# Output projections as split one-pass products, and stick-breaking sums in the scores' bank

## The reference, cut to what matters

```python
# block one, two layers
h = h + 0.5 * g1 * swiglu(mod(norm(h)), ffn1_w_in, ffn1_w_out)
z = mod(norm(h)) @ w_in
mixed = concat([o_a, o_b, o_c, o_d])     # differential attention, convolution, gMLP, forgetting attention
h = h + g2 * (mixed @ w_out)             # phase "o"
h = h + 0.5 * g3 * swiglu(mod(norm(h)), ffn2_w_in, ffn2_w_out)
# block two, two layers
proj = norm(x) @ w_in                    # q, k, v of 24 heads and three gates
y_a, y_b, y_c = o_a @ w_out_a, o_b @ w_out_b, o_c @ w_out_c      # phase "y"
merged = gates[0] * y_a + gates[1] * y_b + gates[2] * y_c
x = x + merged @ w_o                     # phase "wo"
x = x + square(relu(norm(x) @ w_up)) @ w_down
# heads c0 to c5 of block two: stick-breaking, over the keys before each query
z = q @ k.T * scale
a = exp(log_sigmoid(z) + suffix_sum(log_sigmoid(-z)))
```

## Time and profile before

| what | value |
|---|---|
| median of the runs | 2153.49 us (2151.41 to 2154.36) |
| the profiled execution's own time | 2152.88 us |
| its span | 2151.1 us |
| TensorE busy | 2051.2 us, 95% |
| mean granted TensorE clock | 0.974 of 2.4 GHz |
| GpSimd busy | 1332.5 us, 62% |

### The profile page before, as it was taken

One profiled execution on the slowest core, in us unless ns is written; L12 is line 12 of the kernel. 1 busy time (PEld: TensorE's weight loads), 2 busy tenths in 40 slices (PEclk: granted clock), 3 DMA queues, 4 the chain that ended last, 5 costly groups with the idle time before them and its releaser, 6 DMA issues.

```text
span 2151.1 us, 36602 instructions
## 1 busy us (share of the span) xinstructions
PE 2051.2 (95%) x15510; PEld 1966.5 (91%) x15510; DVE 930.2 (43%) x1761; ACT 917.4 (43%) x1393; POOL 1332.5 (62%) x612
## 2 busy tenths in 40 slices
PE   7999997999989999889999999999999999999998
PEld 4999996899989998769998999989999999988998
DVE  4554776561455477754124422144233432134223
ACT  2443454334444335434444354514544345514543
POOL 1778660477967786217887765505896765405885
PEclk8999998999989999999999999999999999999999
DMA  9997550785689775227555543335554543335552
GB/s 326 357 332 253 186 161 20 254 289 176 195 275 349 244 245 167 79 84 250 177 162 170 170 146 116 103 126 166 186 194 134 192 143 113 118 118 168 185 196 79
DMA packets 356787, 398.18 MB, mean 185 GB/s; under 512 B 8984, under 2 KB 318992, under 8 KB 356624
## 3 DMA queue, kind: packets, MB, share of 16 engines
q1 hardware_dynamic: 356464, 395.65, 55.5%
q10 hardware_dynamic: 160, 0.20, 0.0%
HBM read 394.77 MB, written 1.05 MB: 184 GB/s over the span
## 4 chain that ended last, share of the span: by engine, by line
PE 90%; DVE 5%; ACT 3%; SPq 1%; issue 1%; DMA 1%; DVEq 0%; ACTq 0%
PE bank L706 73%; PE bank L783 5%; PE bank L1108 3%; PE bank L938 1%; PE bank L805 1%; PE bank L900 1%; PE bank L1072 1%; SPq L534 1%; DVE arena L1641 1%; ACT arena L1270 1%; PE bank L697 1%; PE bank L999 1%; DVE arena L1685 1%; DMA arena<-in_ada_w 1%; PE bank L939 1%
## 5 line engine op out<-in xcount | busy, mean ns | idle before, releaser
L672 POOL TENSOR_TENSOR w_lo<-ring,w_hi 128x1024 fp32r<-128x1024 f32 (+2 forms) x608 | 1332.3, 2217 | 798.7 <-ACT w_hi L1169 798.1
L706 PE MATMUL bank<-hn,w_hi 128*128 128x256 f32 x2912 | 848.4, 291 | 26.4 <-DVE hn_lo L1578 15.8
L706 PE MATMUL bank<-hn_lo,w_hi 128*128 128x256 f32 x2912 | 832.4, 286 | 0.0
L706 PE MATMUL bank<-hn,w_lo 128*128 128x256 f32 x2912 | 832.1, 286 | 0.0
L1169 ACT ACTIVATE w_hi<-ring 128x1024 fp32r<-128x1024 f32 (+2 forms) x608 | 576.4, 975 | 485.6 <-PE bank L706 356.8
L706 PEld LDWEIGHTS bank<-hn,w_hi 128*128 128x128 f32 x2912 | 567.6, 195 | 36.7 <-issue 34.6
L706 PEld LDWEIGHTS bank<-hn_lo,w_hi 128*128 128x128 f32 x2912 | 567.8, 195 | 4.5 <-issue 3.8
L706 PEld LDWEIGHTS bank<-hn,w_lo 128*128 128x128 f32 x2912 | 567.3, 195 | 0.0
L706 PE MATMUL bank<-gated,w_hi 128*128 128x256 f32 x1408 | 249.7, 280 | 0.0
L706 PEld LDWEIGHTS bank<-gated,w_hi 128*128 128x128 f32 x1408 | 215.0, 187 | 0.0
L706 PE MATMUL bank<-gated,w_lo 128*128 128x256 f32 x704 | 196.4, 279 | 0.0
(11 more groups left out here) (188 smaller groups left out, 2130.1 us busy)
## 6 DMA issues: line engine op xcount, KB each, us to landing
ring<-in_ffn_w_in SPq DMA_DIRECT2D x88, 1024.0 KB, 6.1
ring<-in_w_in SPq DMA_DIRECT2D x72, 1024.0 KB, 5.1
arena<-in_ada_w SPq DMA_DIRECT2D x35, 2048.0 KB, 10.3
ring<-in_w_up SPq DMA_DIRECT2D x32, 1024.0 KB, 5.4
ring<-in_w_down SPq DMA_DIRECT2D x32, 1024.0 KB, 5.0
ring<-in_ffn_w_out SPq DMA_DIRECT2D x32, 768.0 KB, 4.4
ring<-in_ffn_w_out SPq DMA_DIRECT2D x32, 640.0 KB, 4.0
ring<-in_w_in SPq DMA_DIRECT2D x16, 512.0 KB, 3.6
```

The costliest lines, as they stand in the source:

```text
L672: pool.tensor_tensor(w_lo[:, q, ks], ring[:, r, k0:k0 + n], w_hi[:, q, ks], ALU.subtract) \
L706: last = mm(out, a, b, start=start and i == 0, stop=stop and i == 2)
```

## The change

- The phases o, y and wo become split products. Their chunks join the sequence of split chunks: ScalarE rounds them (8 half chunks more a phase) and GpSimd subtracts; `plain_product` goes, and `output` and `y_product` come.
- Their activations get high and low parts. In block one `mix` tiles 0 to 5 are split in pairs (`mix_high` on ScalarE, `mix_low` on VectorE) into `hn`, `hn_lo`; the outputs of fox heads and of all block two heads go from their bank to the high part by ScalarE (`pair_high`) and the low part by VectorE (in place of the copy). `merged` stays in the first branch's bank; ScalarE writes its high part (`merged_high`), VectorE its low part.
- In o and wo the first chunk goes k-tile by k-tile, and waits for each k-tile's parts. Chunks o 0 and o 1 are rounded at steps 2 and 3 of block one's heads. Wo uses banks 6, 7 and 0, 1.
- The gates are opened in two groups between the roundings of y.
- A stick head's suffix sums are added to its first scores, in banks 2 to 5 in turn; the second issue of the scores goes.

```diff
-for _part, _phases in (("one", ("f1in", "f1out", "z", "f2in", "f2out")), ("two", ("z2", "up", "dn"))):
+for _part, _phases in (("one", ("f1in", "f1out", "z", "o", "f2in", "f2out")),
+                       ("two", ("z2", "y", "wo", "up", "dn"))):
...
-            h.sb = [take("two banks", 2, f"sp {h.name}")]
+            h.sb = [take("stick banks", 4, f"copied {h.name} 0")]
             h.tp = [take("tp", SLOTS, f"sp {h.name}"), take("tp", SLOTS, f"arg {h.name}")]
-            h.pb = [take("pb", 2, f"copied {h.name} 0")]
...
+            def output(phase, i, outs, done, free=(), ready=None):
+                q = split_slot(phase, i)
+                for half, (k0, n) in enumerate(halves(phase, i)):
+                    half_ready(phase, i, half)
+                    steps = [(c, k) for k in range(n) for c in range(2)] if ready \
+                        else [(c, k) for c in range(2) for k in range(n)]
+                    for c, k in steps:
...
+                        if ready and c == 0:
+                            ready(kx)
+                        last = terms(outs[c], w_hi[:, q, half * 4 + k, ws], w_lo[:, q, half * 4 + k, ws], hn[:, kx],
+                                     hn_lo[:, kx], False, kx == 0, kx == KT - 1)
...
             def turned(hd, q, k, tile):
                 if hd.kind == "stick":
-                    (qi, ki, _, _), (pb, free) = hd.maps[0], hd.pb[0]
-                    if free:
-                        pe.wait_ge(done_by(free), eng.at(free))
-                    b, sp_ = bank[:, pb], tile[:, hd.tp[1][0], :]
-                    stick_scores(b, q, k, qi, ki, False)
+                    b, sp_ = bank[:, hd.sb[0][0]], tile[:, hd.tp[1][0], :]
                     pe.wait_ge(vector_done, eng.at(f"sp {hd.name}"))
...
+                def mix_ready(k):
+                    mark = {0: "mix parts 0", 2: "mix parts 1", 4: "mix parts 2", 6: "heads d0 2", 7: "heads d0 3"}.get(k)
...
+                def y_product(i):
+                    q = split_slot("y", i)
+                    if i == 0:
+                        pe.wait_ge(scalar_done, eng.at("z2 out 29"))
+                    if i >= 2:
+                        pe.wait_ge(vector_done, eng.at(f"merged parts {i - 2}"))
...
+                def merged_ready(k):
+                    if k % 2 == 0:
+                        pe.wait_ge(vector_done, eng.at(f"merged parts {k // 2}"))
...
+            def pair_high(heads, i, dst):
+                hd = heads[i]
+                if hd.half == 0 or hd.kind == "diff":
+                    return
+                act.wait_ge(tensor_done, eng.at(f"out {hd.name}"))
+                b = bank[:, 6 + hd.pair % 2].rearrange("p (a s) -> p a s", a=2)
+                for a in range(2):
+                    f(dst(hd)[64 * a:64 * a + 64], b[64 * a:64 * a + 64, a], ACT.Copy) \
+                        .then_inc(scalar_done, eng.step(f"high {heads[0].name} {hd.pair}" if a else None))
...
                 def between(i):
+                    if i == 0:
+                        mix_high(2, "mixed out")
+                    if i in (2, 3):
+                        round_chunk("o", i - 2)
+                    if i == 9:
+                        mix_high(0, "od normed")
...
+                        mix_high(1, "conv done")
...
+                    if i + 1 == len(Z2_BETWEEN) - 1:
+                        round_chunk("y", 0)
...
+                round_chunk("y", 1)
+                act.wait_ge(scalar_done, eng.at("z2 out 29"))
+                open_gates(0)
+                open_gates(1)
+                round_chunk("y", 2)
+                open_gates(2)
+                open_gates(3)
+                round_chunk("y", 3)
+                merged_high(0)
+                round_chunk("wo", 0)
+                merged_high(1)
+                round_chunk("wo", 1)
+                merged_high(2)
+                merged_high(3)
+                round_chunk("wo", 2)
+                round_chunk("wo", 3)
...
+                def mix_low(t):
+                    dve.wait_ge(scalar_done, eng.at(f"mix high {t}"))
+                    two = slice(2 * t, 2 * t + 2)
+                    tt(hn_lo[:, two], mix[:, two], hn[:, two], ALU.subtract).then_inc(vector_done, eng.step(f"mix parts {t}"))
+
                 def between(i):
+                    if i == 1:
+                        mix_low(2)
...
+                        mix_low(1)
+                        mix_low(0)
...
                     dve.wait_ge(scalar_done, eng.at(f"gate {i}"))
...
+                    dve.wait_ge(weights_used, eng.at(f"half used y {i}"))
+                    tt(total, total, gate[0], ALU.mult).then_inc(vector_done, eng.step())
+                    dve.wait_ge(weights_used, eng.at(f"used y {i}"))
+                    for br in (1, 2):
...
+                    dve.wait_ge(scalar_done, eng.at(f"merged high {i}"))
+                    two = slice(2 * i, 2 * i + 2)
+                    tt(hn_lo[:, two], total, hn[:, two], ALU.subtract).then_inc(vector_done, eng.step(f"merged parts {i}"))
```

More of the change, by code:

```diff
@@ L337, in place_heads @@
 def place_heads(heads):
[L340 to L341 removed]
+    n = {"two banks": 0, "four banks": 0, "stick banks": 0, "tp": 0, "pb": 0, "ps": 0}
+    banks = {"two banks": (2, 3), "four banks": (2, 3, 0, 1), "stick banks": (2, 3, 4, 5), "pb": (4, 5)}
     last = {}
@@ L768, in out_product @@
                                 last.then_inc(tensor_done, eng.step(done))
[L770 to L777, removed]
+            def output(phase, i, outs, done, free=(), ready=None):
[5 more added lines that the diff above has]
+                    for c, k in steps:
+                        kx, ws = k0 + k, slice(c * P, (c + 1) * P)
+                        if kx == 0:
                             for by, mark in free[c:c + 1]:
                                 pe.wait_ge(by, eng.at(mark))
[L780 to L787, removed]
+                        if ready and c == 0:
+                            ready(kx)
+                        last = terms(outs[c], w_hi[:, q, half * 4 + k, ws], w_lo[:, q, half * 4 + k, ws], hn[:, kx],
+                                     hn_lo[:, kx], False, kx == 0, kx == KT - 1)
+                        if kx == KT - 1 and c == 0:
                             last.then_inc(tensor_done, eng.step(done))
+                    last.then_inc(weights_used, eng.step(f"used {phase} {i}" if half else
+                                                         f"half used {phase} {i}", weights_used))
             def norm_sum(n):
@@ L1100, in _ @@
                     if i >= 2:
[L1101 to L1105, removed]
-                        for c in range(2):
[L1107 to L1111, removed]
@@ new lines, in y_product @@
+                    for half, (k0, n) in enumerate(halves("y", i)):
+                        half_ready("y", i, half)
+                        for c in range(2):
+                            for k in range(k0, k0 + n):
+                                br = 0 if k < 2 else 1 if k < 5 else 2
+                                if i == c == 0 and k in (0, 2, 5):
+                                    pe.wait_ge(vector_done, eng.at(f"heads a0 {(1, 4, 7)[br]}"))
+                                ws = slice(c * P, (c + 1) * P)
+                                b = bank[:, 3 * (i % 2) + br].rearrange("p (c s) -> p c s", c=2)
+                                last = terms(b[:, c], w_hi[:, q, k, ws], w_lo[:, q, k, ws], o2[:, k], o2_lo[:, k],
+                                             False, k in (0, 2, 5) and c == 0, k in (1, 4, 7) and c == 1)
+                        last.then_inc(weights_used, eng.step(f"used y {i}" if half else f"half used y {i}", weights_used))
@@ L1297, in attention @@
                     after(i)
+                    for j in range(len(heads)):
+                        if j + lag(heads, j) + 1 == i:
+                            pair_high(heads, j, dst)
             def copy_row(c):
@@ L1694, in pair_out @@
                 b = bank[:, 6 + hd.pair % 2].rearrange("p (a s) -> p a s", a=2)
+                if hd.kind != "diff":
+                    dve.wait_ge(scalar_done, eng.at(f"high {heads[0].name} {hd.pair}"))
                 for a in range(2):
-                    dve.tensor_copy(dst(hd)[64 * a:64 * a + 64], b[64 * a:64 * a + 64, a]) \
-                        .then_inc(vector_done, eng.step(f"heads {heads[0].name} {hd.pair}" if a else None))
+                    r = slice(64 * a, 64 * a + 64)
+                    if hd.kind == "diff":
+                        i = dve.tensor_copy(dst(hd)[r], b[r, a])
+                    else:
+                        high, low = dst(hd)
+                        i = tt(low[r], b[r, a], high[r], ALU.subtract)
+                    i.then_inc(vector_done, eng.step(f"heads {heads[0].name} {hd.pair}" if a else None))
             tap = [0]
```

101 lines of the change are left out of this document (49 added, 52 removed).

## The result

The changed kernel takes 2184.3 us (2182.66 to 2186.75), the kernel before 2153.9 beside it: ratio 1.0145, 95% interval 1.013 to 1.016. It is slower by 30 us, where 22 were forecast. Its profiled span is 2181.3 us against 2151.1.

A forecast was written before the change was run, and what follows sets the result against it. TensorE, busy 95% of the span, was taken to bound the kernel. From 2152.88 us, block two's +5.25 and block one's +5.8 a layer, twice both, gave +22.1: 2175 us; own range 2160 to 2188, 8 in 10 2143 to 2194.

The forecast's parts named there:

- stick-breaking: Block two's stick heads: the second issue of scores, 0.83 us, goes from twelve heads; -5.0 us a layer, taken in full.
- pairs' way out in block two's heads: Block two's heads: two ScalarE copies and two VectorE subtractions a pair, TensorE waiting in the first steps; +1.2 us a layer.
- y and wo with the stalls, no clock: Block two's y and wo: three stalls from ScalarE's queue give 10.35 of 11.4 us back; -0.95 us a layer.
- the slow clock behind them: Block two's y and wo: granted clock 0.50 behind the three stalls; +5 us a layer, bounds 0 to 10.
- wo to up; the clock behind it: Bubble after wo: VectorE's squares held by GpSimd's subtractions, +4 us a layer; longer slow clock, +1.
- block one's heads, start of o: Early roundings and subtractions of o 0 and o 1 lengthen the heads, +5 us a layer; o starts later, +1.6.
- products of o: Block one's o: 29.71 us now, 23.0 + 1.5 after with split products; -5.2 us a layer.
- o to f2; the clock behind it: Bubble after o: last square later behind GpSimd's subtractions, +2.7 us a layer; slow clock, +1.7.
- Rival (d): All six split phases: TensorE waits for GpSimd's second halves, 2.4 us; inside the forecast's own range, no separate chance.
- Rival (c): Slower still, 2199 us: every stall meets the slow clock, line 1679 held up, stick saving not realized; chance 0.15.

## Why the prediction was right, and where it was off

The sign, the order of size and the places held; 22 us were forecast and 30.4 measured, inside the range. That the sum came this near is in part luck: in the profiled execution up and dn of block two's first layer ran 3.9 us shorter for no known reason, and without that its span would have grown by some 34. By the steps of the prediction, us in the first layer of each block:

| step | forecast | traces |
|---|---|---|
| stick-breaking | -5.0 | -4.9 |
| pairs' way out in block two's heads | +1.2 | about 0 |
| y and wo with the stalls, no clock | -0.95 | -2.2 |
| the slow clock behind them | +5 | +5.7 |
| wo to up; the clock behind it | +4; +1 | +4.9; not to be parted |
| block one's heads, start of o | +5 +1.6 | +12.5 |
| products of o | -5.2 | -4.4 |
| o to f2; the clock behind it | +2.7; +1.7 | +5.5; +0.1 |

In block one's second layer the heads and the start of o cost 11.0, the products of o gave 5.2, just as forecast, and the bubble cost 5.5.

**Y and wo.** ScalarE's queue was walked entry by entry, and its timeline in the changed kernel is that walk:

```profile
1427.28 1.28 ACT L1194 ACT_TABLE_LOAD   x1
...
1430.49 3.22 ACT L1488 ACTIVATE arena<-arena 128x512 f32<-128x512 f32 x6
...
1438.64 1.99 ACT L1177 ACTIVATE w_hi<-ring 128x1024 fp32r<-128x1024 f32 x2
1440.65 0.60 ACT L1492 ACTIVATE hn<-bank 128x512 fp32r<-128x512 f32 x1
```

The stalls were 4.14, 2.36 and 2.64 us where 4.7, 2.55 and 3.1 were forecast, 9.1 in all for 10.35. The 48 matmuls behind each took 2.3, 1.7 and 1.8 us too long, where I took 5 for the clock in all. Rival (d), that TensorE waits for GpSimd's halves, is out: no wait of TensorE in the changed kernel's trace ends at GpSimd, and with ScalarE's order mended y runs without a gap.

**The term that was too small: block one's heads.** It was put at +6.6 us a layer and measured 12.5 and 11.0. I counted four scalings as held for up to 2.4 us, from the row of L1685, took them as partly hidden, and left the operations of L1679 (L1739 after the change) out, since no row of before showed them held. The timeline of VectorE in the changed kernel, with GpSimd's beside it:

```profile
348.66 2.41 DVE L1733 TENSOR_SCALAR stat<-stat,small 128x2 f32<-128x2 f32 x1
...
353.47 2.33 DVE L1739 SCALAR_TENSOR_TENSOR arena<-arena,stat 128x128 f32<-128x128 f32 x1
...
358.18 0.49 DVE L1739 SCALAR_TENSOR_TENSOR arena<-arena,stat 128x256 f32<-128x256 f32 x1
...
348.68 9.31 POOL L671 TENSOR_TENSOR w_lo<-ring,w_hi 128x1024 fp32r<-128x1024 f32 x4 [25.17 <-ACT w_hi L1177]
```

Four subtractions in a row, and four operations of VectorE held for one each, whatever their size, two numbers a partition or 256 (the chain above has all four). Five operations that take 1.8 us by themselves took 10, in a stretch where VectorE was already the busiest engine, and the slow clock came on top. The price was one GpSimd instruction for each VectorE operation in the shadow. The Trainium skill (SBUF — State Buffer, section SBUF: two separate sides) says that the two engines take their shared ports for a whole instruction, also against operations with two SBUF inputs. The row of L1739 agrees (2.33 us under GpSimd, 0.35 without), and my sum would have been up to 2 us a layer nearer with it. Rival (c) had this hold as one of its three parts; of the other two, stick-breaking was realized in full and the clock behind the stalls of y and wo cost 5.7 us, not 10.

**The bubbles.** The mechanism was right, and in o its size was twice what I took. The clock that I put behind it did not come on top in the first layer, where f2's first 288 matmuls took 36.34 us, as before 36.28. In the second it did in part: they took 37.38 us, with a granted clock of 0.70 in the first 10 us, where the first layer has 0.82. Cutting GpSimd's work takes nearly all of the longer bubble away. In o the lag had gathered through the whole phase, nearly every square and some of the sums held for a GpSimd instruction, as the chain shows from 396.89 on.

**Not forecast.** The table's right column gives +13.7 for block one (from z's end to f2 it is 13.6 in the first layer and 11.3 in the second) and +3.5 for block two; there z2's first 96 matmuls took 13.36 us instead of 14.22 in the first layer, so that z2 to up grew by 2.6 and 2.8. That is 30.3, the span's whole growth. What else moved cancels: up and dn of block two's first layer are 3.9 us shorter (below), and 1.5 us came ahead of block one's heads, 0.8 behind its second o and 1.6 in the last layer.

## What to carry to other kernels

Before a change moves work onto GpSimd, count VectorE's operations on SBUF operands in its shadow and price each at one GpSimd instruction, however small it is itself; put the shadow where VectorE works from PSUM or idles. When an engine with a queue in order gets new work, walk its queue and put what another engine waits for ahead of what itself waits; here three calls moved ahead were worth 25.7 us, the stalls themselves and, for a third of y and wo's loss, the clock that fell behind them. A cheaper product is worth its saving only if its operands' preparation has cover: o gave 4.4 us in the first layer and cost 10 even in its best order here (the last half chunk behind the norm: 5.8 in the heads, 3.4 before f2 and 0.9 in f2's first matmuls). Y and wo, split in the same way, gained 11.9 us once the queue's order was right.

## What the runs showed of the hardware

- An instruction of two elements a partition (0.23 to 0.30 us) took 2.41 us beside GpSimd's subtraction. In wo, under subtractions of the same size, the addition with a PSUM input (L2027) kept 0.41 us.
- Three-term products run faster in one place than elsewhere. In the changed kernel's first layer of block two the down projection needs 0.34 us for three matmuls, in its second layer and in the other traces 0.353, with a clock of 1.00 in both. In equal slices of 40 us, the first layer, then the second:

```profile
1580.00:1620.00 40.00, 40.00 (x350) 40.00 (x349) 13.22 (x13) 18.94 (x22) 36.84 (x17) 1.00 0.61 203
...
2090.00:2130.00 40.00, 40.00 (x342) 40.00 (x341) 15.07 (x12) 15.01 (x15) 36.05 (x16) 1.00 0.58 190
```

It makes up and dn 181.6 us long instead of the 184.3 to 185.5 of the other traces (183.6 in the second layer of the kernel before), with the same instructions. Stretches of y in the changed kernel have the faster pace too (16 matmuls in 1.81 us from 1435.80 on). What it comes from stays open; no run here tests it.
